# Expert rows fetched by indirect transfers and transposed, in place of one-hot products, in a two-layer RWKV-7 and sparse-attention decoder

## What is computed

```
def hier_moe(h, ln_g, w_gr, b_gr, w_er, b_er, w1, w3, w2):
    xf = rms_norm(h, ln_g).reshape(n, c)            # n = 512, c = 1024
    ...
    expert = grp * MOE_EXPERTS_PER_GROUP + ei       # two of 32 experts for each token
    weight = grp_w * ew / jnp.sum(ew, -1, keepdims=True)
    ...
    def expert_block(args):                         # xb: the rows of one expert
        xb, e = args
        return (jax.nn.silu(xb @ w1[e]) * (xb @ w3[e])) @ w2[e]   # 1024 -> 512 -> 1024
    ...
    y = jnp.zeros((n, c), yb.dtype).at[buf_t].add(yb * buf_w[:, None].astype(yb.dtype))
```

## Time and profile before

| | |
|---|---|
| median of 3 runs | 1978.74 us (1971.9 to 1980.13) |
| span of the profiled execution, first to last instruction | 1968.5 us, so 10.2 us of the median lie around the span |
| PE busy in the span, PEld | 1825.3 us (93%), 968.9 us (49%) |
| DVE, ACT, POOL busy | 590.5, 362.3, 151.9 us |
| chain that ended last, by engine | PE 84%, DVE 8%, issue 3%, DMA 3% |
| loop of layer 0, loop of layer 1 | 522 to 986 us, 1472 to 1936 us |
| DMA engines busy in both loops | 9 tenths or more of nearly every slice, 430 GB/s |
| all bytes moved | 503.65 MB, of which the two sets of expert weights are 402.7 MB |

### The profile page before, as it was taken

How to read it: one execution, slowest core, us unless ns; L and a number is a source line. 1 busy time by engine, 2 the same in 40 slices (tenths; PEclk the granted TensorE clock), 3 DMA queues, 4 the chain that set the end, 5 groups by cost and what they waited for, 6 DMA issues and landing times.

```text
span 1968.5 us, 25880 instructions
## 1 busy us (share of the span) xinstructions
PE 1825.3 (93%) x11066; PEld 968.9 (49%) x11066; DVE 590.5 (30%) x1259; ACT 362.3 (18%) x841; POOL 151.9 (8%) x200
## 2 busy tenths in 40 slices
PE   6989988989799999999959997999979999999993
PEld 3334347855554444444444576555455444444441
DVE  5453783452221111111030325655122111111113
ACT  2541113311100000000030112666110000000001
POOL 1044010000000000000010000545000000000001
PEclk9989988999799999999959897999979999999997
DMA  4112128060899999999959302010369999999995
GB/s 203 60 69 58 71 75 194 3 264 1 346 418 430 427 430 432 430 430 429 424 209 178 67 1 108 24 32 12 128 256 377 430 429 429 430 432 431 427 428 210
DMA packets 64817, 503.65 MB, mean 256 GB/s; under 512 B 27066, under 2 KB 27450, under 8 KB 46270
## 3 DMA queue, kind: packets, MB, share of 16 engines
q1 hardware_dynamic: 52158, 476.80, 60.7%
q10 hardware_dynamic: 10240, 16.79, 2.3%
q0 software_dynamic: 2304, 8.39, 1.2%
HBM read 465.23 MB, written 36.72 MB: 255 GB/s over the span
## 4 chain that ended last, share of the span: by engine, by line
PE 84%; DVE 8%; issue 3%; DMA 3%; POOL 1%; ACT 1%; SPq 0%; ACTq 0%; POOLq 0%; DVEq 0%
PE bank L1324 70%; PE bank L1376 5%; PE bank L1890 3%; PE bank L1904 2%; DVE spare L962 2%; DVE arena L963 1%; PE bank L1709 1%; DMA arena<-rel_bias 1%; DVE arena L1205 1%; POOL arena L471 1%; DMA arena<-gram_dram 1%; PE bank L1332 1%; POOL arena L469 0%; PE bank L1484 0%; DVE arena L976 0%
## 5 line engine op out<-in xcount | busy, mean ns | idle before, releaser
L1324 PE MATMUL bank<-arena 128*64 128x512 f32 (+10 forms) x5202 | 1264.3, 543 | 34.0 <-DVE arena L927 9.1
L1324 PEld LDWEIGHTS bank<-arena 128*64 128x64 f32 (+5 forms) x5202 | 493.2, 160 | 684.3 <-issue 653.0
L1324 PEld LDWEIGHTS bank<-const,arena 128*128 128x128 f32 x2048 | 238.1, 195 | 51.2 <-issue 48.7
L1324 PE MATMUL bank<-const,arena 128*128 128x128 f32 x2048 | 249.9, 281 | 2.2 <-DVE const L1091 2.2
L1161 DVE TENSOR_TENSOR arena<-arena,bank 128x256 f32<-128x256 f32 x64 | 27.0, 421 | 427.9 <-ACT arena L713 427.9
L719 ACT ACTIVATE arena<-bank 128x512 f32<-128x512 f32 x64 | 38.2, 597 | 426.1 <-PE bank L1324 420.4
L713 ACT ACTIVATE arena<-bank 128x256 f32<-128x256 f32 x64 | 24.5, 383 | 468.4 <-PE bank L1324 468.4
L514 POOL DMA_INDIRECT arena<-y_rows,ints x16 | 16.1, 1005 | 1200.4 <-DMA y_rows<-arena 1196.2
L1098 DVE TENSOR_TENSOR arena<-bank,vec 128x512 f32<-128x512 f32 x64 | 44.3, 692 | 192.7 <-PE bank L1324 192.7
L529 POOL TENSOR_SCALAR arena<-arena,small 128x128 f32<-128x128 f32 (+3 forms) x128 | 76.5, 607 | 103.1 <-DVE small L1301 103.0
L1170 DVE COPY arena<-bank 128x256 f32<-128x256 f32 x64 | 27.1, 424 | 184.3 <-PE bank L1709 184.3
(11 more groups left out here) (236 smaller groups left out, 967.0 us busy)
## 6 DMA issues: line engine op xcount, KB each, us to landing
arena<-m_w SPq DMA_DIRECT2D x64, 4096.0 KB, 21.9
arena<-m_w SPq DMA_DIRECT2D x64, 2048.0 KB, 20.1
y_rows<-arena ACTq DMA_DIRECT2D x128, 128.0 KB, 10.6
y_rows<-arena SPq DMA_DIRECT2D x2, 3840.0 KB, 31.9
arena<-kv_w SPq DMA_DIRECT2D x1, 6144.0 KB, 18.6
rev_bias<-arena SPq DMA_DIRECT2D x1, 5120.0 KB, 69.5
arena<-a_wk SPq DMA_DIRECT2D x2, 2048.0 KB, 14.9
arena<-a_wr SPq DMA_DIRECT2D x2, 2048.0 KB, 7.7
```

What stands on the lines that cost most here:

```text
L1324: return nc.tensor.matmul(dst, lhsT, rhs, start=start, stop=stop)
```

## The change

1. **Fetch.** Once in each layer POOL stores the normed rows `xn_m` to DRAM (`x_rows`, four transfers of 512 KB), as each block is ready. In the loop PE no longer multiplies `xn_m` by `one_hot`. It makes four products of one column (`row_numbers`), which give each of a pair's 128 slots the number of its token; DVE turns them to integers (`pair_index`), with a number outside the table where a slot is empty; POOL fetches the pair's rows with one indirect transfer (`pair_fetch`, 4 KB a row, three buffers, into the place of `xn_m`), and `gather` transposes them, four 128x128 transposes for each half. Row numbers are made three pairs ahead.
2. **Store.** ACT only copies the result to `yb`. POOL stores it with one indirect transfer for each expert (`result_store`, 2 KB half-rows), with a row number outside the table for an empty slot.
3. **Zeros.** Since empty slots are no longer stored, SP clears the whole of `y_rows` in the RWKV stage, and not its overflow part alone: 8 MB more for each layer.
4. **Order.** Ahead of the loop, the row numbers of three pairs come before the first gather.

The diff, cut to its core:

```diff
+        pair_rows = region(1).rearrange("p (s c) -> p s c", s=4)
...
+                sp.dma_start(y_rows[l][0:E * CAP, :].rearrange("(p q) c -> p q c", p=P),
+                             spread(zero_rows, 1, E * CAP // P)).then_inc(sem("y_clear"), 16)
             sp.wait_ge(sem("pe_s"), 7)
-            sp.wait_ge(sem("y_clear"), 32)
+            sp.wait_ge(sem("y_clear"), 64)
...
+                i = 1 + 2 * l
+                for j in range(NJ):
+                    pool.wait_ge(sem("xn_ready"), 4 * i + j - 1)
+                    pool.dma_start(x_rows[l][P * j:P * j + P, :], xn_m[:, j, :]).then_inc(sem(f"x_rows_out{l}"), 16)
+                pool.wait_ge(sem(f"x_rows_out{l}"), 64)
+                pool.wait_ge(sem("tr_done"), 8 * i + 8)
+                def pair_fetch(n):
+                    pool.wait_ge(sem("rows_ready"), at("rows_ready", n + 1))
+                    if n % 16 >= 3:
+                        pool.wait_ge(sem("gathered_T"), at("gathered_T", 2 * n - 4))
+                    nc.gpsimd.indirect_dma_start(
+                        out=pair_rows[:, n % 3, :], out_offset=None, in_=x_rows[l],
+                        in_offset=bass.IndirectOffsetOnAxis(ap=pair_rows_i[:, n % 4:n % 4 + 1], axis=0),
+                        bounds_check=T - 1, oob_is_err=False).then_inc(sem(f"pair_in{n % 3}"), 16)
+                def result_store(n):
+                    pool.wait_ge(sem("yb_ready"), at("yb_ready", n + 1))
+                    nc.gpsimd.indirect_dma_start(
+                        out=y_halves[l], out_offset=bass.IndirectOffsetOnAxis(ap=store_i[:, n % E:n % E + 1], axis=0),
+                        in_=yb[:, n % 2, :], in_offset=None,
+                        bounds_check=2 * SLOTS - 1, oob_is_err=False).then_inc(sem(f"y_store{n % 2}"), 16)
+                for n in range(16 * l, 16 * l + 3):
+                    pair_fetch(n)
+                pool.wait_ge(sem("y_clear"), 64)
+                pool.wait_ge(sem("store_rows"), l + 1)
+                for e in range(E):
+                    n = E * l + e
+                    if e % 2 and e < E - 6:
+                        pair_fetch(n // 2 + 3)
+                    result_store(n)
...
-                        act.wait_ge(sem("yb_ready"), at("yb_ready", n + 1))
-                        for q in range(2):
-                            act.dma_start(y_rows[l][CAP * e:CAP * e + CAP, 512 * q:512 * q + 512],
-                                          yb[CAP * q:CAP * q + CAP, n % 2, :]).then_inc(sem(f"y_store{n % 2}"), 16)
...
-                        dve.wait_ge(sem("gathered_T"), at("gathered_T", 2 * n - 2))
+                        dve.wait_ge(sem("rows_mm"), at("rows_mm", n - 1))
...
+                def pair_index(n, b=1):
+                    dve.wait_ge(sem("rows_mm"), at("rows_mm", n + 1))
+                    if n % 16 >= 4:
+                        dve.wait_ge(sem(f"pair_in{(n - 4) % 3}"), 16 * ((n - 4) // 3 + 1))
+                    nc.vector.tensor_scalar(pair_rows_i[:, n % 4:n % 4 + 1], bank[b][:, 256:257], float(NO_ROW), None,
+                                            ALU.add).then_inc(sem("rows_ready"), 1)
...
+                def store_rows():
+                    then(nc.vector.tensor_scalar(store_f, count, cst("slot"), float(NO_SLOT), ALU.is_le, ALU.mult))
+                    then(nc.vector.scalar_tensor_tensor(store_f, cst("iota")[:, 0:32], float(2 * CAP), store_f, ALU.mult, ALU.add))
+                    nc.vector.tensor_scalar(store_i, store_f, cst("half_row"), None, ALU.add).then_inc(sem("store_rows"), 1)
...
                 pick_tokens(16 * l)
+                pick_tokens(16 * l + 1)
+                pair_index(16 * l, 0)
+                pick_tokens(16 * l + 2)
+                pair_index(16 * l + 1, 1)
                 nc.vector.tensor_copy(count, bank[5][:, 128:160])
                 then(nc.vector.tensor_copy(position, bank[5][:, 0:128].rearrange("p (j n) -> p j n", j=NJ)))
+                pair_index(16 * l + 2, 0)
                 for q in range(2):
                     x_out(16 * l, q)
-                pick_tokens(16 * l + 1)
...
+                def row_numbers(n, b=1):
+                    pe.wait_ge(sem("one_hot"), at("one_hot", n + 1))
+                    if n % 16 >= 2:
+                        pe.wait_ge(sem("rows_ready"), at("rows_ready", n - 1))
+                    for j in range(NJ):
+                        last = mm(bank[b][:, 256:257], one_hot[:, n % 2, j, :, :].rearrange("p e t -> p (e t)"),
+                                  cst("token_less")[:, j:j + 1], j == 0, j == NJ - 1)
+                    last.then_inc(sem("rows_mm"), 1)
                 def gather(n, q):
-                    pe.wait_ge(sem("one_hot"), at("one_hot", n + 1))
+                    pe.wait_ge(sem(f"pair_in{n % 3}"), 16 * (n // 3 + 1))
                     if n:
                         pe.wait_ge(sem("xgT_ready"), at("xgT_ready", 2 * n - 1 + q))
                     for k in range(4):
-                        for j in range(NJ):
-                            at_k = P * (4 * q + k)
-                            last = mm(bank[2 + q][:, P * k:P * k + P], xn_m[:, j, at_k:at_k + P],
-                                      one_hot[:, n % 2, j, :, :].rearrange("p e t -> p (e t)"), j == 0, j == NJ - 1)
+                        at_k = P * (4 * q + k)
+                        last = nc.tensor.transpose(bank[2 + q][:, P * k:P * k + P], pair_rows[:, n % 3, at_k:at_k + P], ident)
                     last.then_inc(sem("gathered_T"), 1)
...
+                for n in range(3):
+                    row_numbers(16 * l + n, n % 2)
                 for q in range(2):
                     gather(16 * l, q)
...
+                    if e % 2:
+                        pe.wait_ge(sem("rows_ready"), at("rows_ready", 16 * l + min(16, e // 2 + 3)))
+                    if e % 2 and e < E - 6:
+                        row_numbers(n // 2 + 3)
...
+        "slot": row % CAP,
+        "half_row": 2 * (row % CAP) + row // CAP,
+        "token_less": row + P * np.arange(4)[None, :] - NO_ROW,
```

31 lines of the change are left out of this document (19 added, 12 removed).

## The result

The changed kernel took 2010.61 us (median of four runs, 2009.57 to 2014.21), the kernel before, on the same chip, 1975.32 (1969.95 to 1980.13): a ratio of 1.0193, 95% interval 1.0156 to 1.023. Measured again on another chip it was 1999.32 against 1972.28, a ratio of 1.0144 (1.0105 to 1.0183). The forecast was 2004. One of the six runs of a kernel further down, `all_slots`, took 2217.26 us where the other five took 1992.84 to 2013.65; its ratio leaves it out.

The account below looks back on a forecast made before the run. The prediction took the loop's transfers, 15.38 us a turn against PE's 14.74, as the bound. Its terms, 11.4 + 11.6 + 2 = +25 us, gave 2004 us against the median 1978.74, range 1979 to 2032.

Parts of the forecast that it names:

- The sign: Whole kernel: the change makes it slower, by +25 us; chance of slower 0.72.
- PE in the loop, worth nothing: Expert loop: PE's turn falls from 14.74 to 11.9 us but hides beside 15.4 us of transfers, so nothing gained.
- Bytes, +6 a layer: Expert loop: halved stores and fetched rows even out on average, but uneven rows lengthen the weights' stream, +6 us a layer.
- the busiest engine: Loop transfers: loads land when the slowest DMA engine is done; filled rows load some engines more, +4 to +19 us a layer.
- rival (a): Loop and its start: transfers carry the rows evenly and the first fetch is quick; 1981 to 1987 us, chance 20%.
- Start, +6: Start of each layer's loop: the first gather waits for a fetch and hidden starts at low clock, +6 us (0 to 10).
- Zeros, +2: RWKV stage: 16.8 MB more zeros delay the `a_wo` load behind them, 0 to 7 us, taken as +2.
- Ends: Layer ends: layer 0 takes the whole shift, +11.4 us; layer 1 +9.0 after PE's slack, plus +2.6 for POOL's last store.
- (b): Loop transfers: whole blocks of engines carry the rows, or empty slots are moved anyway; +13 us more a layer, 2030, chance 17%.
- (c): Loop transfers: fetched rows cost the weights' stream nothing, halved stores shorten it, -10 us a layer; 1960 us, chance 8%.
- (d): Loop: PE loses its clock at every wait; at most 2.6 us at each layer's end, 2009 us, chance 4%.
- (e): Loop: fetches come late and PE waits for rows, losing one turn, 15 us, in each layer; 2034 us, chance 5%.

Follow-up runs that it names:

- all_slots: The changed kernel with empty slots stored too and without the zeros of the experts' rows: 2000.69 us, ratio 1.0152 to the kernel before.
- light loads: The changed kernel with zeros once behind the scan, loading only 256 of 4096 w2 columns from each layer's fourth expert on: 1857.02 us.
- stores_late: The kernel before with POOL's stores of filled rows, one-hot gather kept, and all zeros written once behind the scan: 1956.14 us, ratio 0.9907.
- the kernel with late zeros: The changed kernel with one result table for both layers, its zeros written once behind the scan: 1979.95 us, 1.0041 of the kernel before.
- before_zeros: The kernel before with only the 16.8 MB of zeros for the experts' rows added: 1978.38 us, ratio 1.0037.

## Why the prediction was right, and where it was not

The sign held, and so did the reason: in the loop the transfers hide what PE saves, and the first fetch delays each start. The total came within 7 us of the first median and 5 of the second. That is in part luck. The two loops were predicted 12 us longer, ends included, and came out 0 and 2 us longer in the two executions; the starts were put 7 to 8 us too low, and the zeros 4 and 14 us too low; and 6 us of the first execution are the fall of the clock, which nothing predicted.

- **PE in the loop, worth nothing: right.** The turn was to be 15.3 to 15.7 us with some 3 us of waiting and a DMA share of 1.00: it is 15.5 on average once the start of three slots is used up, with waits of 4.12 and 0.53 in turns, and 1.01. PE's own 11.9 us are confirmed by the light loads' 12.0. The last w13 of layer 0 lands at 963.29 + 38.0 = 1001.3 and PE starts on it at 1001.41: the slack of 1.3 us is gone.
- **Bytes, +6 a layer: the step that failed is the busiest engine.** The loops came out at -2.6 and +2.5, and -0.7 and +2.3. The stream itself, from the first w13 that waits to the landing of the last, took 970.0 - 529.11 = 440.9 us before and 1001.3 - 560.68 = 440.6 after in layer 0, and 439.8 and 442.4 in layer 1, where 6 more were forecast in each. The averages with which the paragraph began hold: with the halved stores and no fetch (stores_late) it took 432.5 us in layer 0, so the stores gave back 8 (10 by the prediction) and the fetch took 8 (9). In layer 1 up to 2.6 us are left for uneven rows. In 600 to 850 us the queues of the kernel before were busy 95.8% and 4.7%, those of the kernel with late zeros too:

```profile
q1 hardware_dynamic: 4732, 102.94, 95.8%
q10 hardware_dynamic: 2708, 4.44, 4.7%
```

```profile
q1 hardware_dynamic: 4706, 102.63, 95.8%
q0 software_dynamic: 2545, 4.40, 4.7%
```

  Weights moved in that stretch fell by 0.3%, 1.4 us in a loop. An uneven dealing that costs 4 to 19 us a layer would show there. The swizzle of the Trainium skill ("DMA: Bandwidth & Descriptors", "The descriptor swizzle"), by which the prediction reckoned +7 and +9 beside its +6, may well be how the rows are dealt; no run here shows it, and the loads did not pay for it. The engines' backlog of three slots, which rival (a) named, is the likely reason; it was not tried apart.
- **Start, +6: right in kind, mis-sized; it is some +9** in every kernel whose first pair is fetched (45.8 to 46.1 us against 37.0 in layer 0, 44.3 to 46.5 in layer 1). The fetch landed 11.2 us after its issue, as the prediction had it. The fetch was issued 4.1 us after the routing's last product (530.91 + 1.75 = 532.7), not 3.1, and the low clock cost hidden of expert 0 9.82 - 7.09 = 2.7 us, not 1.5. These are 2.2 of the missing 3. The 0.6 us that a faster PE was to win back behind it did not come in this piece either.
- **Zeros, +2: the step that failed is where I looked.** I followed the bytes to the next load in their queue and found 0 to 7 us there. They cost nothing there: what SP waited for ahead of `a_wo` was the zeros and then PE,

```profile
SPq L350 <- DMA y_rows<-arena: 41.0, 1, 41.0
SPq L351 <- PE bank L1431: 39.2, 1, 39.2
```

  so the zeros had landed by 427.45 - 39.2 = 388.3 us, not at 412 to 422, and `a_wo` was issued at 427.45, later than the 415 that was named as the limit, because PE was late. They cost in PE, which no semaphore ties to them, +6.2 and +15.6 us in the profiled executions and 6.3 us by the medians of before_zeros. The rows that would have told me were in the trace of before, a timeline row and a stretch beside its own 7.7 MB of zeros:

```profile
326.94 3.65 PE L1376 MATMUL bank<-arena 32*32 32x32 f32 x84 [3.98 <-issue]
...
320.00:340.00 20.00, 16.02 (x219) 12.53 (x216) 4.77 (x9) 3.36 (x7) 0.95 (x1) 0.66 0.87 211
```

  One stop of 3.98 us, and a clock of 0.66 in the 20 us around it. Moving these zeros alone gave 7 us.
- **Ends: nearly right for layer 0, wrong for the last store.** The start's 8.9 us arrived at layer 0's collecting but for 2.6 us, which are the loop's -2.6: 1.4 from PE's slack ahead of the last w13, and 1.1 behind it. In layer 1 PE's slack of 2.4 us was used up, as forecast, by a stream that took 2.6 longer; then the last turn lost 12.22 - 10.52 = 1.7 us to the low clock. The last store by POOL was issued at 1976.88 and the collecting began at 1980.20, 3.3 us later, as before (1937.4 and 1940.57). An indirect store of filled rows does not take the 6.2 us of an indirect fetch.
- **Rivals.** (a) holds for the bytes and not for the start. (b) is excluded by all_slots: empty slots are skipped, worth 6 us a layer. (c), loops 10 us shorter and the sum with them, is not seen. (d) happened every second turn; inside the loop it cost nothing, and at a layer's end 0, 1.7, 2.9 and 1.6 us in the four layers profiled of the changed kernel, where it was put at 2.6 at most. (e) did not happen: after the first, no fetch is waited for.

The Trainium skill ("TensorE: Matmul & The Clock Gate", "HAM oscillation — how this bites in real kernels") has a loop that starts every tile at the low clock after its wait. Here hidden takes 9.73 us behind the wait of 4.12 us and 7.09 behind that of 0.53, so it is every second tile.

## What to carry to other kernels

Where PE and the transfers are within a few per cent of each other, taking work from one buys nothing until the other gives way: 2.7 us of 14.7 came off PE's turn and the loop stayed, while the same edit under lighter loads was worth 82.5 us a layer (461.85 to 379.3). Charge a large background transfer to the engines that run beside it too, not only to what queues behind it: look for stops for "issue" in the trace and for the clock after them, and put the transfer where the busy engine is waiting anyway. And an index that must pass through a transfer ahead of the first product is paid at every start, so let the first tile take the old way (5.4 of the 9 us came back).

## What the runs showed of the hardware beside that

- The scan took 100.40 to 100.42 us in six kernels without zeros beside it, and 107.9 to 125.9 in seven executions with them. A good part of what two executions of one kernel differ by sits there.
- PE's granted clock can fall to half while PE is busy without a gap: 0.53 over 200 to 220 us in one execution and 1.00 in the other, same code, same DMA share of 0.25. The seven of thirteen profiled executions that had such a fall reached the scan 5 to 14 us later than the six others. Its cause stays open.
- Storing all 64 rows of every expert cost the loop the same by ACT in blocks and by POOL in rows of 2 KB under an index, within 1.2 us. Indices outside the table moved no bytes: with them the indirect queue moved 29.39 MB, with every slot stored 37.76 MB, in the same 13184 packets.
